# Slots of second experts from the top, retention's last units later, and x held in DRAM while the experts run

## The reference, cut to what matters

```python
x = x + concat(retention(norm(x)), window_attention(norm(x))) @ w_out
hn = rmsnorm(x, norm2_g)
g_sel = argmax(hn @ w_group)                        # one of 4 groups
top_p, top_i = top_k(softmax(el_of_group), 2)       # 2 of its 8 experts
for e in range(32):
    a = silu(hn @ w_gate[e]) * (hn @ w_up[e])       # 1024 -> 256
    out += comb[:, e] * (a @ w_down[e])             # 256 -> 1024
x = x + out
```

## Time and profile before

| what | us |
|---|---|
| median of 3 runs | 602.77 (602.13 to 603.56) |
| profiled execution | 602.91 |
| its span, first to last instruction | 601.1 |
| PE busy in the span | 512.5 (85%) |
| DVE busy | 249.9 (42%) |
| ACT busy | 145.2 (24%) |
| POOL busy | 151.0 (25%) |
| DMA | 144.75 MB, mean 241 GB/s |
| chain that ended last | PE 44%, SP's issues 23%, DVE 14% |

### The profile page before, as it was taken

How to read it: one execution, slowest core, us unless ns; L and a number is a source line. 1 busy time by engine, 2 the same in 40 slices (tenths; PEclk the granted TensorE clock), 3 DMA queues, 4 the chain that set the end, 5 groups by cost and what they waited for, 6 DMA issues and landing times.

```text
span 601.1 us, 7856 instructions
## 1 busy us (share of the span) xinstructions
PE 512.5 (85%) x2906; PEld 324.2 (54%) x2906; DVE 249.9 (42%) x583; ACT 145.2 (24%) x365; POOL 151.0 (25%) x287
## 2 busy tenths in 40 slices
PE   2686898899999999899995499999877897778895
PEld 2674776677777677568884463334333332233343
DVE  1857768868532465652325522122111111111337
ACT  3552344535545322231211100111000000000110
POOL 4154746203214544640302112112111001100000
PEclk9988999799999999989998589999999988888999
DMA  8512021013004942235936959999999999999885
GB/s 248 193 38 65 19 89 53 2 33 109 2 1 136 334 154 72 70 137 221 401 126 244 414 188 401 415 419 422 419 419 421 418 422 419 420 421 416 357 318 176
DMA packets 35031, 144.75 MB, mean 241 GB/s; under 512 B 5842, under 2 KB 8994, under 8 KB 23216
## 3 DMA queue, kind: packets, MB, share of 16 engines
q1 hardware_dynamic: 27440, 131.58, 56.0%
q0 software_dynamic: 4528, 9.01, 4.2%
q10 hardware_dynamic: 3024, 3.64, 1.8%
HBM read 138.16 MB, written 17.30 MB: 259 GB/s over the span
## 4 chain that ended last, share of the span: by engine, by line
PE 44%; SPq 23%; DVE 14%; issue 5%; ACT 3%; DMA 3%; POOL 2%; ACTq 0%; DVEq 0%; POOLq 0%
PE banks L970 17%; SPq L668 13%; SPq L676 6%; PE banks L1194 6%; SPq L749 3%; DMA w_moe_a<-in_w_up_dram 3%; PE banks L1209 2%; PE banks L964 2%; PE banks L1028 2%; POOL w_lo L816 1%; PE banks L1147 1%; PE banks L1113 1%; PE banks L1108 1%; PE banks L1188 1%; PE banks L1282 1%
## 5 line engine op out<-in xcount | busy, mean ns | idle before, releaser
L816 POOL TENSOR_TENSOR w_lo<-w_raw,w_hi 128x512 fp32r<-128x512 f32 x52 | 69.1, 1346 | 130.6 <-ACT w_hi L1453 129.0
L1194 PE MATMUL banks<-w_moe_b,xgT 128*64 128x512 f32 x224 | 71.7, 657 | 18.1 <-DMA w_moe_b<-in_w_up_dram 10.8
L1194 PE MATMUL banks<-w_moe_a,xgT 128*64 128x512 f32 x224 | 70.2, 642 | 8.4 <-DMA w_moe_a<-in_w_up_dram 8.4
L2062 DVE SCALAR_TENSOR_TENSOR glu<-banks,wr,glu 128x256 f32<-128x256 f32 x15 | 7.2, 483 | 125.4 <-ACT glu L1585 125.4
L970 PE MATMUL banks<-w_hi,xT_hi_a 128*128 128x512 f32 (+3 forms) x124 | 51.6, 416 | 7.6 <-ACT sv L1408 7.6
L862 POOL DMA_INDIRECT y_d<-y_sb,idx x14 | 14.1, 1005 | 169.1 <-PE banks L1188 112.0
L1194 PEld LDWEIGHTS banks<-w_moe_b,xgT 128*64 128x64 f32 x224 | 22.4, 151 | 60.1 <-issue 59.7
L970 PE MATMUL banks<-w_lo,xT_hi_a 128*128 128x512 f32 (+3 forms) x124 | 49.2, 397 | 0.0
L970 PE MATMUL banks<-w_hi,xT_lo_a 128*128 128x512 f32 (+3 forms) x124 | 48.8, 393 | 0.0
L1585 ACT ACTIVATE glu<-banks,wr 128x256 f32<-128x256 f32 x15 | 7.1, 474 | 157.2 <-PE banks L1194 140.0
L2026 DVE TENSOR_TENSOR xgT<-banks,g_both 128x1024 f32<-128x1024 f32 x16 | 19.5, 1225 | 52.9 <-PE banks L1188 52.9
(11 more groups left out here) (297 smaller groups left out, 914.7 us busy)
## 6 DMA issues: line engine op xcount, KB each, us to landing
w_moe_a<-in_w_down_dram SPq DMA_DIRECT2D x20, 1024.0 KB, 24.8
w_moe_a<-in_w_gate_dram SPq DMA_DIRECT2D x16, 1024.0 KB, 23.3
w_moe_a<-in_w_up_dram SPq DMA_DIRECT2D x16, 1024.0 KB, 27.6
w_moe_b<-in_w_gate_dram SPq DMA_DIRECT2D x14, 1024.0 KB, 18.6
w_moe_b<-in_w_up_dram SPq DMA_DIRECT2D x14, 1024.0 KB, 21.2
w_moe_b<-in_w_down_dram SPq DMA_DIRECT2D x12, 1024.0 KB, 25.2
w_raw<-in_w_in_dram SPq DMA_DIRECT2D x36, 256.0 KB, 4.5
y_d<-in_consts_dram SPq DMA_DIRECT2D x9, 512.0 KB, 10.3
```

The source lines that it names most:

```text
L816: nc.gpsimd.tensor_tensor(w_lo[:, s, :], w_raw[:, s, :], w_hi[:, s, :].bitcast(F32), ALU.subtract).then_inc(split, 1)
L1194: l = mm(acc[64 * e:64 * e + 64, u, :].rearrange("p (m f) -> p m f", m=2), xgT[:, xu, k, 64 * e:64 * e + 64], units(at_e[e], 2)[:, :, k * ...
```

## The change

It does four things. (1) `slots` takes the place of `iota` when slots are assigned: the odd expert of a pair is filled from partition 127 downwards. The constant's columns take the place of `ones`, and DVE makes the ones of `counting` from `ident`. (2) Norm and transposes of retention's units 6 to 9 stand at slots 11, 12, 13, 14 of the list and no longer at 10, 11, 12, 12. (3) `x_sb` shares its place with `w_moe_x`, two units that take pair 0's down matrices. They are loaded once hn_d is written and the router's transposes and squares have read x; x is read back from hn_d in five transfers behind the last pair's down, and DVE's first use of it waits for them (`x_in`). The ring keeps 18 units; pair 1's downs stand where pair 0's stood, and every later pair's downs one place earlier. `oh_last` lies over another unit, the last pair has the same pattern as the others, and some waits on SP change with this. (4) The first product of the last rows (`last_rows(0, 0)`) stands in the middle of the last gate-up and no longer behind it.

```diff
 NUNIT = UNITS_A + UNITS_B
-FIN_UNIT, OVER_UNIT, YTOK_UNIT = 12, 6, 6
+FIN_UNIT, OVER_UNIT, YTOK_UNIT, OH_UNIT = 12, 6, 6, 4
 LAST = NPAIR - 1
...
     behind[done(RG, TAIL)].append(("gate2", TAIL))
-    late = [3, 4, 5, 6, 7, 8, 10, 11, 12, 12]
+    late = [3, 4, 5, 6, 7, 8, 11, 12, 13, 14]
     for m, (t, par) in enumerate(RUNITS):
...
     put("before", p[:, None] < p[None, :])
-    put("ones", np.ones((P, P)))
+
+    put("slots", np.tile(np.where(p < CAP, p, P + CAP - 1 - p) + 1, (P, 1)))
     put("iota", np.tile(p + 1, (P, 1)))
...
-        ident, iota, ones = const("ident"), const("iota"), const("ones")
+        ident, iota, slots = const("ident"), const("iota"), const("slots")
         cos_t = const("cos").rearrange("p (t d) -> p t d", t=NT)
...
         with nc.sbuf_tensor("x_sb", [P, NT, D], F32) as x_sb:
+            pass
+
+        with nc.sbuf_tensor("w_moe_x", [P, 2, KD * FF], F32) as w_moe_x:
             pass
...
+        with nc.sbuf_tensor("units_ahead_oh", [P, OH_UNIT, KD * FF], F32):
+            with nc.sbuf_tensor("oh_last", [P, 2, NT, P], F32R) as oh_last:
+                pass
         w_moe_a = sb("w_moe_a", [P, UNITS_A, KD * FF])
...
             with nc.sbuf_tensor("y_last", [P, 2, 2, D], F32R) as y_last:
-                with nc.sbuf_tensor("oh_last", [P, 2, NT, P], F32R) as oh_last:
-                    pass
+                pass
         w_moe_b = sb("w_moe_b", [P, UNITS_B, KD * FF])
...
         def gu_unit(p, e):
-            return (0 if p == 0 else 6 * p - 2 if p < LAST else 6 * p) + 2 * e
+            return max(6 * p - 2, 0) + 2 * e
...
             return 2 * m + e if p == 0 else gu_unit(p, e) + m
-
-        def dn_unit(p, e):
-            return (6 * p + 8 if p < LAST - 1 else 6 * p + 4) + e
...
             return w_moe_a[:, i:i + n, :] if i < UNITS_A else w_moe_b[:, i - UNITS_A:i - UNITS_A + n, :]
+
+        def dn_at(p, e):
+            return w_moe_x[:, e, :] if p == 0 else units(6 * p + 2 + e, 1)[:, 0, :]
...
                 for e in range(2):
-                    sp.dma_start(units(dn_unit(p, e), 1)[:, 0, :], down_v[2 * p + e]).then_inc(dn_in[p % 4], 16)
+                    sp.dma_start(dn_at(p, e), down_v[2 * p + e]).then_inc(dn_in[p % 4], 16)
...
             load_gu(1)
-            load_dn(0)
+            load_dn(1)
...
             load_gu(2)
-            load_dn(1)
-            for p in range(3, LAST):
-                for e in range(2):
-                    if p > 3:
-                        sp.wait_ge(gu_ps, p - 2)
-                    elif e:
-                        sp.wait_ge(gate_ps, 1)
-                    load_gu_of(p, e)
-                if p > 3:
+
+            sp.wait_ge(hn_out, 16 * NT)
+            sp.wait_ge(hT_ps, 2 * NT)
+            sp.wait_ge(sq2, 2 * NT)
+            load_dn(0)
+            load_gu_of(3, 0)
+            load_dn(2)
+            sp.wait_ge(gate_ps, 1)
+            load_gu_of(3, 1)
+            sp.wait_ge(gu_ps, 1)
+            load_dn(3)
+            for p in range(4, LAST):
+                sp.wait_ge(gu_ps, p - 2)
+                load_gu(p)
+                if p > 4:
                     sp.wait_ge(y_ps, p - 3)
-                else:
-                    sp.wait_ge(gu_ps, 1)
-                load_dn(p - 1)
+                    load_dn(p - 1)
+            sp.wait_ge(y_ps, LAST - 3)
+            load_dn(LAST - 1)
             sp.wait_ge(gu_ps, LAST - 2)
-            load_dn(LAST - 1)
-            sp.wait_ge(y_ps, LAST - 3)
             for half, landed in enumerate((first_half, gu_in[LAST % 4])):
...
                                      ).then_inc(landed, 16)
-            sp.wait_ge(gu_ps, LAST - 1)
+            sp.wait_ge(y_ps, LAST - 2)
             load_dn(LAST)
+
+            for t in range(NT):
+                n = out_rows(t)
+                sp.dma_start(x_sb[0:n, t, :], hn_d[P * t:P * t + n, :]).then_inc(x_in[t], 16)
...
-            def down(at_e):
+            def down(mats):
                 for n in range(2):
...
                             l = mm(acc[64 * e:64 * e + 64, 2 + n, :], actT[:, j, 64 * e:64 * e + 64],
-                                   units(at_e[e], 1)[:, 0, j * D + n * 512:j * D + n * 512 + 512],
+                                   mats[e][:, j * D + n * 512:j * D + n * 512 + 512],
                                    start=(j == 0), stop=(j == 1))
...
                             l = mm(acc[64 * e:64 * e + 64, 2 + n, :], actT[:, j, 64 * e:64 * e + 64],
-                                   units(dn_unit(p, e), 1)[:, 0, j * D + n * 512:j * D + n * 512 + 512],
+                                   dn_at(p, e)[:, j * D + n * 512:j * D + n * 512 + 512],
                                    start=(j == 0), stop=(j == 1))
...
                     pe.wait_ge(y_ev, p)
-                down([dn_unit(p, e) for e in range(2)]).then_inc(y_ps, 1)
+                down([dn_at(p, e) for e in range(2)]).then_inc(y_ps, 1)
...
                         pe.wait_ge(L_ye, it + 1)
-                        down((OVER_UNIT + 4, OVER_UNIT + 5)).then_inc(L_y, 1)
+                        down([units(OVER_UNIT + 4 + e, 1)[:, 0, :] for e in range(2)]).then_inc(L_y, 1)
                 pe.wait_ge(L_ye, NPAIR * (LEVELS - 1) + 1)
...
                 if k == KD // 2:
+                    pe.wait_ge(oh_fin, 1)
+                    last_rows(0, 0, first=True)
                     pe.wait_ge(gu_in[LAST % 4], LAST // 4 * 64 + 64)
...
             l.then_inc(gu_ps, 1)
-            pe.wait_ge(oh_fin, 1)
-            last_rows(0, 0, first=True)
             act_T_of(LAST)
...
                 lo = at["before"][0]
-                step(nc.vector.tensor_copy(counting[:, :, :].rearrange("p a n -> p (a n)"), cst[:, lo:lo + 2 * P]))
+                step(nc.vector.tensor_copy(counting[:, 0, :], cst[:, lo:lo + P]))
+                step(ts(counting[:, 1, :], ident, 0.0, 1.0, ALU.mult, ALU.add))
                 step(ts(small[:, 100:108], iota[:, 0:8], -OFF, None, ALU.add))
...
             for h in range(2):
-                tt(row_oh[:, NT * h:NT * h + NT, :], iota.unsqueeze(1).to_broadcast([P, NT, P]),
+                tt(row_oh[:, NT * h:NT * h + NT, :], slots.unsqueeze(1).to_broadcast([P, NT, P]),
                    row_l[:, NT * h:NT * h + NT].unsqueeze(2).to_broadcast([P, NT, P]), ALU.is_equal
...
                 one(tt(row_l[:, :], lvl_a[:, :], lvl_b[:, :], ALU.mult))
-                one(tt(row_oh[:, :, :], iota.unsqueeze(1).to_broadcast([P, 2 * NT, P]),
+                one(tt(row_oh[:, :, :], slots.unsqueeze(1).to_broadcast([P, 2 * NT, P]),
                        row_l[:, :].unsqueeze(2).to_broadcast([P, 2 * NT, P]), ALU.is_equal))
...
                 dve.wait_ge(yg_in[t], 32)
+                dve.wait_ge(x_in[t], 48 if t < TAIL else 64)
                 step(tt(x_sb[0:R, t, :], x_sb[0:R, t, :], y_tok(t, k)[0:R, :], ALU.add))
...
             n_most = dve.value_load(most_i[0:1, 0:1], min_val=0, max_val=T_TOK)
```

## The result

Four executions of each on the same chip: before 602.45 us, after 610.66 us (medians), ratio 1.0136 with a 95% interval of 1.0105 to 1.0167. The profiled execution took 610.55 us, its span 608.8. So the change costs 8.2 us where the prediction had +1.1, and the result lies outside the range of 600.0 to 608.0.

The account below looks back on a forecast made before the run. The expert part was taken to end when the weight stream ends. Terms: -3.5 + 2.5 - 4.2 + 5.8 - 0.7 + 1.2 = +1.1 us on 602.91, forecast 604.0 us, range 600.0 to 608.0.

Parts of the forecast that it names:

- Retention, -3.5: Up to the router: moving the last units' transposes later shortens TensorE's waits and avoids half clock, 3.5 us gained, bounds 0 and 6.9.
- Gathers, +2.5: Start of the experts: the second gather meets the extra prefetched weights and TensorE waits, 2.5 us lost, bounds 0 and 4.2.
- Prefetch, -4.2: Weight stream: two extra downs load while queues stood still, pair 5's first matrix lands 4.2 us earlier, bounds 0 and 5.0.
- Reload, +5.8: Behind the last pair's downs: x's 2.36 MB go in ahead of y's reads, 5.8 us, from 5.6 up to 6.6.
- 0.7 of slack: Tail: about half of VectorE's 1.40 us wait for TensorE hides a later y, 0.7 us, bounds 0 and 1.4.
- 1.2 of clock: Tail: TensorE stands some 3 us before y's first tile, half clock follows, 1.2 us lost, bounds 0 and 1.7.
- Slots, 0: Second experts' slots filled from the top: same operations and rows, the heaviest queue as heavy, 0 us, bounds -1 to +5.
- the upper bound, 6.6: Reload of x before y: its cost priced by y's own reads instead of 420 GB/s, up to 6.6 us.
- B: Rival, weight stream: the prefetch gives nothing, the 4.2 is missing, 608.2 us, or 606 with better retention; chance 0.12.
- C: Rival, slots: the queue with the doubled rows is the slower one, stream ends up to 5 us later, 609; chance 0.08.

Follow-up runs that it names:

- the hold: Kernel after, with pair 2's downs held back on SP until the second gather has landed: 607.67 us, ratio 1.0078 to the kernel before.

## Why the prediction was wrong

Step by step, the prediction's term first, then what the traces and runs show.

- **Retention, -3.5:** -1.8 in the pair of traces, -2.3 (-0.8 to -3.8) in the runs. The bounds held, the middle was too much. The waits did not shrink but moved: 1.28, 0.98 and 1.85 us where the earlier trace rows had 2.07, 0.90 and 0.55, together 4.1 instead of 3.5. What was gained is the clock: it falls in one place (4 us at 0.57, so 1.7 us lost) instead of two (3.4). That gives 1.1. The other 0.8 are not retention's: after is that much ahead already at 243.53 us (the kernel before reaches the same matmuls, L1071 there and L1085 here, at 244.34), ahead of the first step that was moved. In the trace with retention alone the same holds: 1.4 us at the first gather, of which 0.3 are there at 244.07. So retention itself gave 1.0 and 1.1 us in the traces, and the rest of the -1.8 is chance.

```profile
249.40 0.65 PE L1085 MATMUL banks<-rv,rqk 128*64 128x128 f32 x4 [1.28 <-DVE ret_aT L1828]
...
254.75 0.44 PE L1139 MATMUL banks<-cst,o_rows 128*128 128x128 f32 x2 [0.98 <-DVE o_rows L1879]
...
259.80 0.44 PE L1139 MATMUL banks<-cst,o_rows 128*128 128x128 f32 x2 [1.85 <-DVE o_rows L1879]
```

```profile
253.00:258.00 5.00, 3.96 (x18) 2.64 (x16) 3.80 (x10) 1.03 (x3) 2.31 (x11) 1.00 0.14 39
260.00:264.00 4.00, 4.00 (x14) 3.06 (x13) 2.52 (x5) 0.93 (x2) 1.28 (x1) 0.57 0.00 0
```

- **Gathers, +2.5:** 3.4, and the hold gave back 3.5 in the runs (3.0 in the traces). The mechanism was right, the landing too (10.8 us, foreseen 10.1 to 10.9); the size was off because the clock stays at its lower level through the transposes and into gate-up. It stood in the bounds as 1.7 us and should have been in the middle.
- **Prefetch, -4.2:** -2.9. The place (pair 5's issue, the pause from 378) was right, and so was the first landing: the first matrix of pair 5 lands 9.3 us after its issue in the kernel before and 4.7 in after (by the arrivals of its sixteen parts, the last at 385.0; 5.5 in the run with the hold), where the prediction had 9.6 and 5.4. But of these 4.6 us only 2.9 are left when the last down lands. What took the 1.7 in between was not traced; the prediction took the gain at the first landing for the gain at the end.
- **Reload, +5.8, less 0.7 of slack, plus 1.2 of clock:** this step failed. 9.0 us in the trace, 10.4 in the run that adds it alone. Slack and clock together came to nothing: the tail from y's first tile takes 18.9 us in both kernels, though the granted clock was 0.53 from 584 to 590. That makes the reload 9.0 against 5.8. The error was to price x by its bytes at 420 GB/s. The five reads are not alike: the tile of 64 rows runs at half speed where the queues are in it together, and as they are far apart at that point (the first of the sixteen parts of x's first read arrives at 563.2 us, the last at 576.8), the leading ones are in it while the last ones still have x's first tiles before them. On the last queue x's five reads take 7.7 us instead of 5.6. Then the leading queues come to y's own tiles of 64 rows (their first parts arrive at 584.8) while the last ones have y's first tile, which takes 3.9 us instead of 2.5. That the packets of other tiles grow longer is measured (of 552 packets of 4 KB that start between 572 and 580 us 28% take over 250 ns, and x's tile of 64 rows has only 64 packets); that it is the sharing of ports which does it is argued from the page. The trace of before had the warning: the upper bound, 6.6, came from y's ten reads (4.72 MB from 576.3 to 589.3 us, so 6.5 for x's half of the bytes), and was set aside without asking why these take longer than their bytes. They hold two tiles of 64 rows.
- **Slots, 0:** right within what can be told.
- **Rivals:** none of them describes what happened. B's and C's prices would have come near the result for reasons that the traces and runs exclude: pair 5's first matrix landed at 385.0 and not at 388, the prefetch gave 2.9 and not 0, and the slots cost no 5 us. That no rival asked whether the reload could cost more than its bytes is why the range ended at 608.

With the traces' own sizes in the prediction's sum, 602.9 - 1.8 + 3.4 - 2.9 + 9.0 = 610.6, which is what the profiled execution took, as it must be: the four sizes are differences between the same two traces. What supports them from outside are the runs: 2.3, 3.5 and 10.4 us for the first, the second and the last.

## What to carry to other kernels

Data that is taken out of SBUF for a prefetch has to come back on the queue that bounds the kernel; price its return where it lands, between the last weight and the first operation of the tail, and compare that to what the prefetch can give at most. A prefetch that stands ahead of the transfers that start the work can delay these, and it may cost nothing to let them pass first. When the DMA share is full, read the GB/s beside it: here a full share with half the bytes was a transfer that was slow by its shape, and transfers behind it paid for it.

## What had not been expected

- Transfers into 64 partitions take some 300 ns for a packet of 4 KB where those into 128 take 160, when many queues are in them together (216 against 414 GB/s), and transfers that are under way beside them grow slower too. It is not so on every queue: in after the queue furthest behind took its part of x's tile of 64 rows in at most 0.65 us, 160 ns for a packet.
- Executions of kernels that are the same up to the router (but for one small instruction with the slots) issue the first gather at 335.57, 337.54, 338.45 and 339.86 us (the reload, the slots, the kernel before, the reload without the first tile). A single pair of traces tells no difference of 2 us in that part; what retention gave rests on the runs. All traces together agree with them: on average the first gather is issued at 338.0 us in the six without the later units and at 336.0 in the ten with them. What makes the executions differ was not looked into.
- Also not tried: how far the queues are apart without the scatters, and whether y's two reads of 64 rows, joined into one of 128 partitions, would shorten the tail.
